# A trunk of two layers on one core: three weight loads of the time mixing wait for the key products

## The reference

```
xx = pad(x)[:, :-1] - x                     # token shift
xr, xk, xv = x + xx*mu_r, x + xx*mu_k, x + xx*mu_v
r, k, v = xr @ w_r, xk @ w_k, xv @ w_v      # receptance, key, value
w, a, g = low-rank functions of x + xx*mu   # decay, rate, gate
kk = normalised(k * k_k);  k = k * (1 + (a - 1) * k_a);  b = kk * a
state = state * w_t + (state @ -kk_t) b_t + v_t k_t     # for each token
y_t = state @ r_t
out = (groupnorm(y) + bonus(r, k, v)) * g @ w_out
```

## Time and profile before

| what | before |
|---|---|
| time of the runs, us | 1274.49, 1278.8, 1283.93 |
| profiled execution, us | 1283.47 |
| its span, us | 1281.7 |
| TensorE (PE) busy | 1152.0 us, 90% |
| VectorE (DVE) busy | 934.2 us, 73% |
| ScalarE (ACT) busy | 555.7 us, 43% |
| mean granted clock of TensorE | 0.928 |
| data moved | 252.88 MB, mean 197 GB/s |

### The profile page before, as it was taken

One profiled execution on the slowest core, in us unless ns is written; L12 is line 12 of the kernel. 1 busy time (PEld: TensorE's weight loads), 2 busy tenths in 40 slices (PEclk: granted clock), 3 DMA queues, 4 the chain that ended last, 5 costly groups with the idle time before them and its releaser, 6 DMA issues.

```text
span 1281.7 us, 20232 instructions
## 1 busy us (share of the span) xinstructions
PE 1152.0 (90%) x7950; PEld 921.5 (72%) x7950; DVE 934.2 (73%) x1242; ACT 555.7 (43%) x797; POOL 9.7 (1%) x27
## 2 busy tenths in 40 slices
PE   5799999898788999989999996699788867999998
PEld 1588888686466888877788885467668856788886
DVE  5878887688968888877888885787791785544553
ACT  2534443545844444455444443574332122633341
POOL 1000000000000000000000000000000000000000
PEclk7999999889798999999999997898895788999999
DMA  9788887472228889865788977124413021655540
GB/s 328 262 305 297 295 295 255 138 262 66 66 68 314 270 302 326 301 236 199 264 292 293 317 266 183 34 82 125 161 51 85 24 80 54 211 196 197 196 164 33
DMA packets 185852, 252.88 MB, mean 197 GB/s; under 512 B 30449, under 2 KB 121585, under 8 KB 185777
## 3 DMA queue, kind: packets, MB, share of 16 engines
q1 hardware_dynamic: 181554, 251.32, 58.2%
q10 hardware_dynamic: 4224, 0.52, 0.3%
HBM read 249.71 MB, written 2.10 MB: 196 GB/s over the span
## 4 chain that ended last, share of the span: by engine, by line
PE 70%; DVE 16%; DMA 5%; issue 4%; ACT 3%; SPq 2%; POOL 0%; DVEq 0%; ACTq 0%; POOLq 0%
PE bank L703 20%; PE bank L705 20%; PE bank L704 20%; DVE ada_acc L1814 3%; DVE gu_lo L1886 2%; DMA ada_raw<-in_ada_w_dram 1%; DMA front<-in_ada_w_dram 1%; PE bank L1174 1%; PE bank L765 1%; PE bank L1059 1%; DVE dn_lo L1896 1%; ACT gu_hi L1308 1%; PE bank L712 1%; DVE probs L2426 1%; DMA raw<-in_ffn_w_gu_dram 1%
## 5 line engine op out<-in xcount | busy, mean ns | idle before, releaser
L703 PE MATMUL bank<-gu_hi,xT_hi 128*128 128x512 f32 (+1 forms) x944 | 376.2, 398 | 22.4 <-DVE gu_lo L1886 9.1
L705 PE MATMUL bank<-gu_hi,xT_lo 128*128 128x512 f32 (+1 forms) x944 | 372.9, 395 | 0.0
L704 PE MATMUL bank<-gu_lo,xT_hi 128*128 128x512 f32 (+1 forms) x944 | 372.7, 395 | 0.0
L1886 DVE TENSOR_TENSOR gu_lo<-raw,gu_hi 128x2048 fp32r<-128x2048 f32 (+1 forms) x108 | 239.6, 2253 | 17.5 <-ACT gu_hi L1308 17.4
L703 PEld LDWEIGHTS bank<-gu_hi,xT_hi 128*128 128x128 f32 x944 | 181.6, 192 | 66.7 <-issue 17.5
L704 PEld LDWEIGHTS bank<-gu_lo,xT_hi 128*128 128x128 f32 x944 | 181.4, 192 | 39.1 <-issue 0.7
L705 PEld LDWEIGHTS bank<-gu_hi,xT_lo 128*128 128x128 f32 x944 | 181.3, 192 | 38.2
L1308 ACT CAST gu_hi<-raw 128x2048 fp32r<-128x2048 f32 (+1 forms) x108 | 200.2, 1882 | 19.4 <-DMA raw<-in_rwkv_w_rkv_dram 8.3
L1814 DVE SCALAR_TENSOR_TENSOR ada_acc<-ada_raw,cact,ada_acc 128x512 f32<-128x512 f32 x224 | 168.4, 752 | 12.3 <-DMA ada_raw<-in_ada_w_dram 1.8
L703 PE MATMUL bank<-dn_hi,hT_hi 128*128 128x512 f32 x320 | 136.9, 428 | 6.6 <-DVE dn_lo L1896 6.6
L1896 DVE TENSOR_TENSOR dn_lo<-raw,dn_hi 128x2048 fp32r<-128x2048 f32 x40 | 91.7, 2292 | 65.7 <-ACT dn_hi L1319 65.6
(11 more groups left out here) (285 smaller groups left out, 1169.9 us busy)
## 6 DMA issues: line engine op xcount, KB each, us to landing
raw<-in_ffn_w_gu_dram SPq DMA_DIRECT2D x176, 512.0 KB, 9.0
ada_raw<-in_ada_w_dram SPq DMA_DIRECT2D x128, 512.0 KB, 7.1
raw<-in_ffn_w_down_dram SPq DMA_DIRECT2D x40, 1024.0 KB, 5.0
raw<-in_rwkv_w_rkv_dram SPq DMA_DIRECT2D x24, 512.0 KB, 5.0
raw<-in_dsa_w_in_dram SPq DMA_DIRECT2D x16, 512.0 KB, 4.8
front<-in_ada_w_dram SPq DMA_DIRECT2D x8, 512.0 KB, 7.9
last_raw<-in_ffn_w_down_dram SPq DMA_DIRECT2D x4, 1024.0 KB, 5.2
raw<-in_dsa_w_out_dram SPq DMA_DIRECT2D x8, 512.0 KB, 4.8
```

The costliest lines, as they stand in the source:

```text
L703: nc.tensor.matmul(out_ap, sta_hi, mov_hi, start=start, stop=False, skip_group_check=True)
L704: nc.tensor.matmul(out_ap, sta_hi, mov_lo, start=False, stop=False, skip_group_check=True)
L705: return nc.tensor.matmul(out_ap, sta_lo, mov_hi, start=False, stop=stop, skip_group_check=True)
L1886: nc.vector.tensor_tensor(gu_lo[:, par, ks, 0:width], buf[:, i, 0:4 * width].rearrange("p (k c) -> p k c", k=4), gu_hi[:, par, ks, 0:width ...
```

## The change

SP waits, behind the load of `inv_in`, until `pairs_mm` is 2, that is, until TensorE has finished `ak`. Only then does it issue the loads of block 44 half 1 and of block 45. Nothing else is changed.

More of the change, by code:

```diff
@@ L581, in rwkv @@
                 sp.dma_start(inv_in[:].rearrange("p s u -> p (s u)"), inv_dram[0]).then_inc(inv_loaded, 16)
+                sp.wait_ge(pairs_mm, 2)
                 load_half(R_BLOCK, w_r, 0, 1)
```

## The result

Over 20 runs each the changed kernel took 1283.84 us (1280.43 to 1291.07) and the kernel before 1279.87 us (1272.33 to 1284.95). The ratio is 1.0038, 95% interval 1.0021 to 1.0056: slower by 4.9 us, with 2.7 to 7.2 us in the interval. Both are inside 1%, as forecast, but the forecast itself was +0.2 us, with -1 to +2.3 us around it, and the whole interval of the first set, from +2.7 us on, lies above that.

The account below looks back on a forecast made before the run. TensorE's order of work and stops were taken to set the end, with VectorE's inverse chain arriving together at the r products. The stop's 4.4 us gain, taken by the late load, left +0.2 us: 1279.0 us, range 1273 to 1287.

Parts of the forecast that it names:

- The stop (1): Key products on TensorE: the stop shrinks from 6.45 to 2.04 us, so they end 4.4 us earlier, at 903.2.
- Rival A: Key products: the stop is not the loads' doing and stays 6.45 us; +4.6 us, 1283.4 us; chance 0.18.
- Half 0 (2): First projection of block 44 on TensorE: starts at 904.5 after the receptance mix, at the low clock first, ends about 912.1.
- The load (3): Block 44 half 1: transfers issued at 903.3 and 903.7 land at 909.3 after 5.6 us; VectorE idles 4.1 us.
- What VectorE gets back (4): Remainder of block 45 half 1: VectorE's 3.89 us wait vanishes, leaving a net slip of +0.25 us.
- case C: Block 44 half 1's pair takes 7.2 us to load: +2.3 us, 1281.1 us; upper end of the forecast, within its 0.68.
- TensorE (5): TensorE could start the r products 0.9 us sooner but waits for r_scaled(1): start about 952.7, 0.2 us later.
- the rest of SP's queue (6): Gate matrix, output weights and inverse store behind SP's wait: each has over 6 us to spare, so nothing.

Follow-up runs that it names:

- e1: The kernel before, unchanged, for a second profile: stop in the key products 5.2 us, first r product 53.0 us after the first inverse step.
- e10: The kernel before, unchanged, for a third profile: stop 5.6 us, first r product 52.0 us after the first inverse step.
- e6: Against the kernel before, SP waits for the last state product before loading the norm's vectors and last output weights: ratio 1.0004.
- e4: Against the changed kernel, block 44 half 1 is loaded before SP's wait, only block 45 behind it: ratio 0.9991.
- e9: The kernel of e4 again, block 44 half 1 loaded before SP's wait, for a second profile: ratio 0.9998.
- e7: Against the kernel before, the edits of e4 and e6 together, block 45 behind the key products: ratio 0.9987.
- e12: The kernel of e7 again, with the edits of e4 and e6 together: ratio 0.9983, median 1277.49 us against 1279.43 for the kernel before.
- e2: The changed kernel, unchanged, for a second profile and more times: ratio 1.0036 to the kernel before.
- e8: The changed kernel, unchanged, for a third profile: stop 2.3 us, first r product 56.9 us after the first inverse step.
- e11: The changed kernel, unchanged, for a fourth profile: stop 2.1 us, first r product 57.6 us after the first inverse step.
- e3: Against the changed kernel, SP waits for the middle of the key products instead of their end: ratio 1.0023.
- e5: Against the changed kernel, SP waits for the end of block 44 half 0 on TensorE instead of the key products: 1289.61 us, ratio 1.0082.

## Why the prediction was right in its mechanism and short in its size

**The stop (1).** Right. It was priced at 2.04 us; four profiles of the changed kernel have 2.0, 2.0, 2.3 and 2.1. Rival A fell: the stop is the loads' doing. It depends on what is queued when the block is wanted: 5.2 to 7.3 us with the four transfers (before, e1, e10, e6), 2.7 to 3.2 with two (e4, e9, e7, e12), 1.9 to 2.3 with none. In all fourteen profiles the products go on 2.3 to 2.8 us after the start of one packet of q8, and this packet starts 4.7 to 6.6 us after the first key product with four transfers, 1.9 to 2.5 with two, 1.3 to 1.5 with none. So the block is what is late; whether its request or its packet waited, no view shows. That A's price of 4.6 us is near the measured 4.9 is an accident; its mechanism is in no trace.

**Half 0 (2).** Right in the profiled execution: TensorE waited 1.0 us for the mix, and its clock was at 0.50 until about 905.0 (the end of half 0 adds up to 912.0, not 912.1). What it didn't foresee is a second fall: in e2, e8 and e11 TensorE waited 2.8 to 4.6 us for the remainder of half 1, and the granted clock was 0.50 again for 3.4 to 6.8 us (910.5 to 917.3 in e11). In e11 half 1 ran at it, x1(0) and the cast behind it came late, and VectorE waited a further 0.41 us for block 45 half 1.

**The load (3).** Here the sum failed. I took 6.0 us from the first issue to the landing of block 44 half 1 (5.6 us from the second), leaning on the pair of 909.4 in the earlier trace rows, behind which only 0.6 MB of the gate matrix went out. The cast started 6.3, 7.0, 8.3 and 8.3 us after it (for the first one: 898.83 and 905.13), mean 7.5. The second transfer itself took 5.8, 6.5, 7.8 and 7.7 us, mean 7.0. Here four transfers go out together, as with the pair of the earlier trace rows that took 7.2 us; that row, my upper end, was the nearer one. (With the issue at 903.7, 7.2 us give 910.9 and case C +1.9 us; 911.3 and +2.3 come out only with the 0.8 us between the two issues of before.) The issue itself came at 4.8 to 5.5 us after the first inverse step, mean 5.2, where I had 4.8, since the inverse starts 0.1 to 0.8 us ahead of the key products in these traces and not with them.

**What VectorE gets back (4).** The mechanism was right: the wait for block 45 half 1 vanishes. Its size was that of one profile, 3.89 us; four have 3.3 us on average (3.9, 3.0, 2.0 and 4.4, with stops of 6.5, 5.2, 5.6 and 7.3 us).

The three terms: 1.5 us more for the load, 0.4 for the issue, 0.6 less to give back, on 0.25 us: +2.8 us, against the 2.9 us of the table. That is a little beyond case C, the upper end of the forecast, and just inside both intervals of the time. The total of 1279.0 us missed by 4.8: besides, the kernel before has a median of 1279.87 us over 20 runs, not the 1278.8 of three that I built on. That 1283.84 us lies in the stated range, 1273 to 1287, says little, since the range was made wide enough for the scatter and for A.

**TensorE (5) and the rest of SP's queue (6).** Right in the main: TensorE arrives first and waits 1.0, 0.4 and 0.5 us for r_scaled(1) in after, e2 and e8, while in e11, with its slow half 1, no such wait shows. In none of the four does TensorE wait for one of the later loads.

**What stays open.** 4.9 us were measured and 2.9 are shown. The rest, 2 us, may be nothing: the interval begins at 2.7 us, and from the first inverse step to the end of the span three profiles of before took 383.2, 379.2 and 383.6 us and four of the changed kernel 387.9, 381.8, 383.7 and 386.3, which is 2.9 us more in the mean. But e3 (+2.9 us at an unchanged wait) and e4 and e9 (0.3 to 1.2 us gained where the wait gives 2.9) lack about the same 2 to 3 us. Each alone is within its noise or at its edge; together they leave room for a second cost of holding loads back, which nothing here locates. It may also be the clock, which TensorE gets at the bonus matmuls in some executions and not in others. Why the same four transfers land once in 5.5 us (e5) and once in 8.3 was not found.

## What to carry to other kernels

A load that is held back must be weighed against its first reader, not against the engine that the wait relieves: here the shorter code stop gave 4 us to TensorE, while the r products hang on VectorE, which got only the lateness. Hold back the loads with slack and let the one with a near reader through. And look whether the two ends of a stage arrive together, for then a gain on one of them is worth nothing; price a term from several executions where it scatters by as much as the effect.

## What the runs showed of the hardware

A code block comes the later the more data are queued when it is wanted (stops of 2, 3 and 5 to 7 us for none, two and four transfers of 512 KB), though it is a single 16 KB packet. The rise of TensorE's granted clock from 0.50 to 1.00 behind the r products came 27 to 29 us after the first of them in eight executions, 38 to 42 us in five and 55 us in one, and each of three kernels (before, the changed one, e4's) has both an early and a late one. This makes 3 us on 32 matmuls of 251 or 353 ns; two profiles of different kernels can differ by it alone.
